# Moving the second block's modulation product from GpSimd in the mixing stage to VectorE in the first feed-forward and down products

## The chip, the cores and the metric

One core of a Trainium2 chip. The metric is the device time of the kernel in microseconds (us), from several executions of the same program. One further execution is recorded by the hardware profiler; its page and its trace are what is read here. Engines: TensorE (PE in the rows, PEld its weight loads), VectorE (DVE), ScalarE (ACT), GpSimd (POOL), and SyncE (SP), which issues transfers. A difference of 0.2% is about what repeated measurements of this kernel can tell from none.

## The reference

Two transformer blocks, one after the other, on a sequence of 512 tokens and 1024 features, all in float32. What matters here:

```
mod = silu(c) @ w_ada + b_ada            # 1024 x 6144 weight, 25 MB, one row
sh1, sc1, g1, sh2, sc2, g2 = split(mod)  # six vectors of 1024
# second block
h = rms_norm(x, norm1_g) * (1 + sc1) + sh1 ... x = x + g1 * (mixed @ w_out)
h = rms_norm(x, norm2_g) * (1 + sc2) + sh2 ... x = x + g2 * (... @ w_down)
# end of the first block, which needs nothing of mod
f = (silu(h @ w_gate) * (h @ w_up)) @ w_down     # 1024 -> 2816 -> 1024
```

So mod depends on c alone, and its first use is the norm at the start of the second block.

## The kernel before

Features lie on partitions, the 512 tokens along the free axis. Weights come as tiles of 1024 x 128 (128 partitions x 8 slices x 128 columns, 512 KB) through three slots. For each tile SP loads `raw` (helper `load`, line 514), ScalarE writes the high part `w_hi` (`split_hi`, line 1102), VectorE the rest `w_lo` (`split_lo`, line 1578), and TensorE does 24 matmuls of 128x128x512: three products for each of 8 slices (line 619, or 806 in the mixing stage). `load` waits until the slot's previous tile has been split (`split_ready`), `split_hi` waits until TensorE has done with the slot (`unit_done`). SP issues its transfers in the order of its program, and each wait there holds all that stands behind it.

The mixing stage of the first block runs in 8 rounds of four or five tiles (`ROUNDS`). In each round TensorE puts projections between the scores, transposes and value products of a pair of heads, VectorE does the score reductions, splits, reciprocals of the gates and norms, and ScalarE the exponentials. Behind the rounds come the products of branch b (line 927), then w_out, norms, the first feed-forward product, the down product, and the second block.

The modulation runs on GpSimd beside these 8 rounds. w_ada is cut into 96 tiles of 64 output features, with the 1024 inputs as 128 partitions x 8; GpSimd loads a tile through its own queue (`ada_load`, line 470, two buffers), multiplies it by cond (line 479), adds in three halvings (lines 482 and 484) into `ada_acc`, and after 12 tiles signals `ada_ready` (line 488). At the end of each round TensorE waits for that signal (`modulation`, line 881) and sums over the partitions with 6 matmuls against ones (12 passes in the rows) into bank O1; VectorE adds the bias (`modulate_out`, line 1790) and frees the bank, and GpSimd begins the next twelve. cond = silu(c) was made early by ScalarE (line 1141) and VectorE (lines 1671 to 1673), with the 1024 features as 128 x 8. Behind the branch products VectorE makes `mod_a` = (1 + sc) * g (lines 1932, 1933).

The first feed-forward product has 22 gate tiles (slot 0) and 22 up tiles (up 0 in slot 2, the others in slot 1). After a first pair, 21 rounds run as a loop on every engine:
- TensorE: up tile j+1 into bank G1, gate tile j+1 into G0.
- VectorE, round j: wait for G1, `cval` (line 1986), `split_lo(1)` of up tile j+2; wait for G0, `cgate` (line 1989), `split_lo(0)` of gate tile j+2; then `fbuf` (line 1970) and, once ScalarE has made f_hi, `f_lo` (line 1973).
- ScalarE: `split_hi(1)`, `split_hi(0)`, silu (line 1399), `f_hi` (line 1401).
- SP, loop of 20 (`ffn_rounds`): load gate tile j+1, load up tile j+2. The gate load waits for the split of gate j, the up load for that of up j+1.

The down product has 8 output tiles of three weight tiles (slots 1, 0, 2 with 8, 8 and 6 slices), accumulated in O0 and O1 by turns; behind each, ScalarE squares and copies it, and VectorE adds the squares and splits the next tile of slot 2.

The waits are counted with semaphores: `w.next(signal, ahead=1)` waits for one use less than the count so far, and `credit=1` lets the first such wait pass. A buffer guarded so is reloaded only after its previous use.

Of the kernel before, what the change touches and what calls it, by code (L numbers as in the profile page):

```python
# [20 lines left out]
F32 = mybir.dt.float32  # L21
F32R = mybir.dt.float32r
I32 = mybir.dt.int32
ACT = mybir.ActivationFunctionType
# [31 lines left out]
def slopes_table():  # L56
# [9 lines left out]
            ("gla_norm_g_2", 1), ("c_2", 8), ("conv_b_2", 44), ("conv_w_2", 132), ("q_norm_g_2", 1), ("k_norm_g_2", 1)]  # L66
# [96 lines left out]
def build(nc, a, out):  # L163
    with ExitStack() as ctx:
# [18 lines left out]
        def signal(name, unit=1, credit=0):  # L183
# [20 lines left out]
        cond = sb("cond", [8])  # L204
        eps6 = sb("eps6", [1])
        eps5 = sb("eps5", [1])
        lamv = sb("lamv", [4, 64])
# [11 lines left out]
        ada_acc = sb("ada_acc", [12, 64])  # L219
# [28 lines left out]
            ("qk", [2, 2, S], F32), ("probs", [2, CAUSAL], F32), ("ada", [2, 8, 64], F32))  # L248
# [37 lines left out]
        ada_flat = ada_acc[:, :, :].rearrange("p a b -> p (a b)")  # L286

# [22 lines left out]
        cond_exp = signal("cond_exp")  # L310
# [40 lines left out]
        ada_used = [signal("ada_used0"), signal("ada_used1")]  # L351
        cond_r = signal("cond_r")
        ada_mm = signal("ada_mm", credit=1)
        ada_ready = signal("ada_ready")
        ada_out = signal("ada_out", credit=1)
# [78 lines left out]
        def _(pool):  # L434
# [33 lines left out]
            def ada_load(t, n):  # L468

                pool.dma_start(ada[:, n, :, :], a["w_ada"][bass.ds(t, 1), :, :]  # L470
                               .rearrange("t p (k c) -> (t p) k c", k=8)).then_inc(ada_in[n], 16)

            def ada_chunk(c, last=False):
                pool.wait_ge(ada_mm, w.next(ada_mm, ahead=1))
                for n in range(12):
                    buf = n % 2
                    chunk = ada[:, buf, :, :]
                    pool.wait_ge(ada_in[buf], w.next(ada_in[buf]))
                    then(pool.tensor_tensor(chunk, chunk, cond[:, :].rearrange("p (k c) -> p k c", c=1).broadcast_to([P, 8, 64]),  # L479
                                            ALU.mult))  # L480
                    for half in (4, 2):
                        then(pool.tensor_tensor(ada[:, buf, 0:half, :], ada[:, buf, 0:half, :],  # L482
                                                ada[:, buf, half:2 * half, :], ALU.add))
                    pool.tensor_tensor(ada_acc[:, n, :], ada[:, buf, 0, :], ada[:, buf, 1, :], ALU.add).then_inc(ada_used[buf], 1)  # L484
                    pool.wait_ge(ada_used[buf], w.next(ada_used[buf]))
                    if n < 10 or not last:
                        ada_load(c * 12 + n + 2, buf)
                pool.sem_inc(ada_ready, 1)  # L488

            for n in range(2):  # L490
                ada_load(n, n)
            pool.wait_ge(cond_r, w.next(cond_r))
# [15 lines left out]
        def _(sp):  # L508
# [66 lines left out]
            ffn_rounds("w_gate", "w_up", 0, "w_down")  # L575
            down_rounds("w_down")
# [25 lines left out]
        def _(pe):  # L602
            w = Waits(pe)
            for free in (v_turned, ada_mm, *unit_done):
                pe.sem_inc(free, 1)
# [268 lines left out]
            def modulation(i):  # L874

                pe.wait_ge(ada_ready, i + 1)
                pe.wait_ge(ada_out, i + 1)
                if i >= 5:
                    pe.wait_ge(o_rs, min(i - 4, 3) if i < 7 else 4)
                for n in range(6):  # L880
                    last = pe.matmul(O1[:, n:n + 1], ada_flat[:, n * P:(n + 1) * P], ones[:, 0:1], start=True, stop=True)  # L881
                last.then_inc(ada_mm, 1)

            for i in range(8):
# [33 lines left out]
                modulation(i)  # L918
# [170 lines left out]
        def _(act):  # L1089
# [44 lines left out]
            for n in range(4):  # L1134
# [5 lines left out]
                if n == 1:  # L1140
                    act.activation(cond[:, :], cols[:, VEC_AT["c_2"]:VEC_AT["c_2"] + 8], ACT.Exp, scale=-1.0).then_inc(cond_exp, 1)
# [1117 lines left out]
```

## Time and profile before

| | us |
|---|---|
| median of 3 runs | 1629.0 (1628.54 to 1630.68) |
| the profiled execution, its own time | 1627.7 |
| its span in the profile | 1626.0 |
| TensorE busy | 1445.8 (89%) |
| VectorE busy | 860.0 (53%) |
| ScalarE busy | 580.6 (36%) |
| GpSimd busy | 353.9 (22%), all within the first 482 us |
| transfers | 146.19 MB, mean 90 GB/s |
| mean granted clock of TensorE | 0.944 of full speed |

Busy time is a share over stages with different limits; an engine's idle time costs only where the chain that ended last runs through it. The profile lists for each group of instructions the idle time of its engine just before it and what ended that, and for any stretch the busy time of each engine and the granted clock of TensorE. Matmul ends are modelled and overlap the next start, so 0.39 us of duration go with 0.227 from start to start at full clock.

### The profile page before, as it was taken

To read this page: it belongs to the slowest core of one execution; us is meant where nothing else is said; L and a number is where in the kernel's file an instruction comes from. 1 tells how busy PE (TensorE), PEld (TensorE's weight loads), DVE (VectorE), ACT (ScalarE), POOL (GpSimd) and SP (SyncE) were. 2 spreads that over 40 slices of the span, in tenths; PEclk is the share of its full clock that TensorE was granted. 3 is DMA by queue.
4 is the path that set the end of the run, shared out by engine and by line. 5 is a ranking of instruction groups with operands and counts; after the bars stand their busy time and mean duration, and the time that the engine had idled before them with its cause. 6 is when DMAs were issued, how large, how long until landed. Compare 5 with 4: busy or idle time off the path is not lost.

```text
span 1626.0 us, 19342 instructions
## 1 busy us (share of the span) xinstructions
PE 1445.8 (89%) x6538; PEld 1147.0 (71%) x6538; DVE 860.0 (53%) x1299; ACT 580.6 (36%) x917; POOL 353.9 (22%) x511
## 2 busy tenths in 40 slices
PE   7994586668678899999999889989979999999999
PEld 6773464456456678888888668866757788888887
DVE  5863354566457635444422368755554656565321
ACT  5441232233233433232322362444423544444221
POOL 5867777777750000000000000000000000000000
PEclk9996887788789999999999989999999999999999
DMA  5443332333312122222333121211102132323332
GB/s 193 138 126 89 102 110 84 105 110 96 104 54 96 62 90 91 100 93 97 97 107 94 61 79 52 78 39 39 52 13 101 64 103 90 103 91 100 111 94 87
DMA packets 42176, 146.19 MB, mean 90 GB/s; under 512 B 5376, under 2 KB 5648, under 8 KB 42128
## 3 DMA queue, kind: packets, MB, share of 16 engines
q1 hardware_dynamic: 34448, 120.39, 22.4%
q0 software_dynamic: 7680, 25.17, 5.4%
q8 instruction: 29, 0.48, 0.1%
q14 instruction: 19, 0.16, 0.0%
HBM read 143.44 MB, written 2.10 MB: 90 GB/s over the span
## 4 chain that ended last, share of the span: by engine, by line
PE 70%; POOL 15%; issue 7%; DVE 4%; ACT 1%; DMA 1%; POOLq 1%; DVEq 0%; SPq 0%; ACTq 0%
PE bank L619 55%; POOL ada L482 7%; POOL ada L479 5%; PE bank L763 3%; PE bank L654 2%; POOL ada_acc L484 2%; PE bank L806 1%; PE bank L1023 1%; PE bank L881 1%; PE bank L735 1%; PE bank L927 1%; PE bank L669 1%; PE bank L726 1%; PE bank L641 1%; POOL ada L470 1%
## 5 line engine op out<-in xcount | busy, mean ns | idle before, releaser
L1578 DVE TENSOR_TENSOR w_lo<-raw,w_hi 128x1024 fp32r<-128x1024 f32 (+1 forms) x225 | 278.3, 1239 | 199.4 <-ACT w_hi L1102 198.0
L619 PE MATMUL bank<-h_hi,w_hi 128*128 128x512 f32 x872 | 345.6, 396 | 0.8 <-DVE gyf L2122 0.8
L1102 ACT ACTIVATE w_hi<-raw 128x1024 fp32r<-128x1024 f32 (+1 forms) x225 | 233.4, 1039 | 308.1 <-PE bank L619 287.4
L619 PE MATMUL bank<-h_lo,w_hi 128*128 128x512 f32 x872 | 340.4, 390 | 0.0
L619 PE MATMUL bank<-h_hi,w_lo 128*128 128x512 f32 x872 | 340.2, 390 | 0.0
L619 PEld LDWEIGHTS bank<-h_hi,w_hi 128*128 128x128 f32 x872 | 164.0, 188 | 42.2 <-issue 7.1
L619 PEld LDWEIGHTS bank<-h_hi,w_lo 128*128 128x128 f32 x872 | 164.1, 188 | 34.7
L619 PEld LDWEIGHTS bank<-h_lo,w_hi 128*128 128x128 f32 x872 | 164.3, 188 | 32.7 <-issue 0.2
L619 PE MATMUL bank<-f_hi,w_lo 128*128 128x512 f32 x352 | 137.0, 389 | 0.0
L619 PE MATMUL bank<-f_lo,w_hi 128*128 128x512 f32 x352 | 137.0, 389 | 0.0
L619 PE MATMUL bank<-f_hi,w_hi 128*128 128x512 f32 x352 | 137.0, 389 | 0.0
L482 POOL TENSOR_TENSOR ada<-ada 128x256 f32<-128x256 f32 x192 | 131.6, 686 | 15.1
L881 PE MATMUL bank<-ones,ada_acc 128*128 128x1 f32 x96 | 20.4, 340 | 112.5 <-POOLq L488 112.5
L479 POOL TENSOR_TENSOR ada<-ada,cond 128x512 f32<-128x512 f32 x96 | 103.9, 1082 | 25.2 <-PE bank L881 19.5
L806 PE MATMUL bank<-h_hi,w_hi 128*128 128x512 f32 x240 | 102.4, 427 | 0.3 <-DVE ma L1774 0.3
L502 POOL IOTA mj<- 128x128 int32 x1 | 0.2, 234 | 470.2 <-DVE gacc L2020 470.2
L881 PEld LDWEIGHTS bank<-ones,ada_acc 128*128 128x128 f32 x96 | 19.9, 312 | 115.5 <-POOLq L488 115.5
L806 PE MATMUL bank<-h_hi,w_lo 128*128 128x512 f32 x240 | 96.7, 403 | 0.0
L806 PE MATMUL bank<-h_lo,w_hi 128*128 128x512 f32 x240 | 96.6, 403 | 0.0
L1178 ACT ACTIVATE probs<-probs,negmaxs 128x128 f32<-128x128 f32 (+3 forms) x64 | 35.4, 554 | 163.2 <-DVE negmaxs L1723 163.2
L619 PEld LDWEIGHTS bank<-f_hi,w_hi 128*128 128x128 f32 x352 | 66.1, 188 | 13.8
L619 PEld LDWEIGHTS bank<-f_lo,w_hi 128*128 128x128 f32 x352 | 66.1, 188 | 13.7
(297 smaller groups left out, 2188.3 us busy)
## 6 DMA issues: line engine op xcount, KB each, us to landing
raw<-in_w_up SPq DMA_DIRECT2D x66, 512.0 KB, 3.3
raw<-in_w_mix SPq DMA_DIRECT2D x48, 512.0 KB, 3.4
ada<-in_w_ada POOLq DMA_DIRECT2D x96, 256.0 KB, 3.0
raw<-in_w_down SPq DMA_DIRECT2D x32, 512.0 KB, 3.5
raw<-in_w_in SPq DMA_DIRECT2D x25, 512.0 KB, 3.3
raw<-in_w_gate SPq DMA_DIRECT2D x22, 512.0 KB, 3.3
raw<-in_w_out SPq DMA_DIRECT2D x16, 512.0 KB, 3.3
raw<-in_w_down SPq DMA_DIRECT2D x16, 384.0 KB, 3.2
```

The source lines that it names most:

```text
L470: pool.dma_start(ada[:, n, :, :], a["w_ada"][bass.ds(t, 1), :, :] .rearrange("t p (k c) -> (t p) k c", k=8)).then_inc(ada_in[n], 16)
L479: then(pool.tensor_tensor(chunk, chunk, cond[:, :].rearrange("p (k c) -> p k c", c=1).broadcast_to([P, 8, 64]), ALU.mult))
L482: then(pool.tensor_tensor(ada[:, buf, 0:half, :], ada[:, buf, 0:half, :], ada[:, buf, half:2 * half, :], ALU.add))
L484: pool.tensor_tensor(ada_acc[:, n, :], ada[:, buf, 0, :], ada[:, buf, 1, :], ALU.add).then_inc(ada_used[buf], 1)
L619: last = pe.matmul(to[:, :], wt[:, slot, k, :], act_[:, rhs0 + k, :], start=(k == first and n == 0), stop=(k == K - 1 and n == 2))
L654: last = pe.matmul(to[g][:, :], wt[:, slot, k, :], act_[:, k, :], start=(k == 0 and n == 0), stop=(k == KU - 1 and n == 2))
L763: last = pe.matmul(banks[r][:, :], xt[:, k, P * r:P * r + P], wt[:, slot, 4 * kk:4 * kk + 4, :].rearrange("p a b -> p (a b)"), start=(k == ...
L806: last = pe.matmul(G[u % 2][:, :], wt[:, slot, k, :], act_[:, kr, :], start=(kr == 0 and m == 0), stop=(kr == length - 1 and m == 2))
L881: last = pe.matmul(O1[:, n:n + 1], ada_flat[:, n * P:(n + 1) * P], ones[:, 0:1], start=True, stop=True)
L1102: act.activation(w_hi[:, s, 0:K, :], raw[:, s, 0:K, :], ACT.Copy).then_inc(hi_ready[s], 1)
L1178: act.activation(probs[:, m, p:p + P * (r + 1)], probs[:, m, p:p + P * (r + 1)], ACT.Exp, scale=-1.0, bias=negmaxs[:, r, m:m + 1], accum_o ...
L1578: dve.tensor_tensor(w_lo[:, s, 0:K, :], raw[:, s, 0:K, :], w_hi[:, s, 0:K, :].bitcast(F32), ALU.subtract).then_inc(split_ready[s], 1)
```

## The change

The modulation leaves GpSimd, TensorE and the mixing stage. The weight is stored transposed, as 48 blocks of 128 output features x 1024 inputs with the features on partitions, and c is stored broadcast to all partitions (128 x 1024). A block comes in two halves of 128 x 512 (256 KB each), loaded by SP. VectorE takes each half with one product-and-sum instruction against cond and adds the two sums into one column of `modc`. Blocks 0 to 41 go two to a round of the feed-forward loop, blocks 42 to 47 with the first six output tiles of the down product. `ada` has one buffer for each half, and SP's loads of them stand between the tile loads of the same queue. ScalarE makes cond with one Silu. The bias and mod_a are made before the norm behind the down product. In the mixing stage all waits for the modulation go; where bank O1 was freed by them, a wait for `o_rs` stands instead.

```diff
         ada_in = [signal("ada_in0", 16), signal("ada_in1", 16)]
-        ada_used = [signal("ada_used0"), signal("ada_used1")]
+        ada_used = [signal("ada_used0", credit=1), signal("ada_used1", credit=1)]
+        cond_in = signal("cond_in", 16)
...
@@ GpSimd
-            def ada_load(t, n):
-                pool.dma_start(ada[:, n, :, :], a["w_ada"][bass.ds(t, 1), :, :]
...
-            with w.repeat(7, {ada_in[0]: 6, ada_in[1]: 6, ada_used[0]: 6, ada_used[1]: 6, (ada_mm, 1): 1, step: 36}) as c:
-                ada_chunk(c)
-            ada_chunk(7, last=True)
...
@@ SP
-            def ffn_rounds(gate, up, up0, down):
+            def ada_load(t):
+
+                for half in range(2):
+                    sp.wait_ge(ada_used[half], w.next(ada_used[half], ahead=1))
+                    sp.dma_start(ada[:, half, :], a["w_ada"][bass.ds(t, 1), :, half * S:half * S + S]
+                                 .rearrange("t p k -> (t p) k")).then_inc(ada_in[half], 16)
+
+            def ffn_rounds(gate, up, up0, down, modulation=False):
 
                 load(0, tile(gate, 0))
                 load(1, tile(up, up0 + 1))
                 down_unit(down, 0, 2)
-                with w.repeat(NF - 2, {(split_ready[0], 1): 1, (split_ready[1], 1): 1}) as j:
+                more = {}
+                if modulation:
+                    sp.dma_start(cond[:, :], a["c_2"]).then_inc(cond_in, 16)
+                    more = {(ada_used[0], 1): 2, (ada_used[1], 1): 2}
+                with w.repeat(NF - 2, {(split_ready[0], 1): 1, (split_ready[1], 1): 1, **more}) as j:
                     load(0, tile(gate, j + 1))
+                    if modulation:
+                        ada_load(j * 2)
                     load(1, tile(up, j + (up0 + 2)))
+                    if modulation:
+                        ada_load(j * 2 + 1)
                 load(0, tile(gate, NF - 1))
+                if modulation:
+                    ada_load(2 * NF - 4)
 
-            def down_rounds(name):
+            def down_rounds(name, modulation=False):
 
                 down_unit(name, 0, 1)
+                if modulation:
+                    ada_load(2 * NF - 3)
                 down_unit(name, 0, 0)
+                if modulation:
+                    ada_load(2 * NF - 2)
                 for c in range(1, KD):
                     for s in DOWN:
                         down_unit(name, c, s)
+                        if modulation and s == 0 and c <= 5:
+                            ada_load(2 * NF - 2 + c)
...
@@ TensorE, mixing stage
                 pe.wait_ge(o_sq, i - 3)
-                pe.wait_ge(ada_out, min(i + 1, 7) + 1)
+                pe.wait_ge(o_rs, i - 4) if i >= 5 else None
...
-                modulation(i)
...
@@ ScalarE
             gated(0, gate_pre)
+            act.wait_ge(cond_in, w.next(cond_in))
+            act.activation(cond[:, :], cond[:, :], ACT.Silu).then_inc(cond_r, 1)
...
@@ VectorE, mixing stage
-                modulate_out(i)
...
@@ VectorE, feed-forward loop
+            def modulation(t, parity):
+
+                for half in range(2):
+                    dve.wait_ge(ada_in[half], w.next(ada_in[half]))
+                    dve.tensor_tensor_reduce(ada[:, half, :], ada[:, half, :], cond[:, half * S:half * S + S], 1.0, 0.0,
+                                             ALU.mult, ALU.add, ada_sum[:, parity, half:half + 1]).then_inc(ada_used[half], 1)
+                for half in range(2):
+                    dve.wait_ge(ada_used[half], w.next(ada_used[half]))
+                dve.tensor_tensor(modc[:, bass.ds(t, 1)], ada_sum[:, parity, 0:1], ada_sum[:, parity, 1:2],
+                                  ALU.add).then_inc(mod_sum[parity], 1)
...
                 split_lo(1)
+                modulation(j * 2, 0)
                 dve.wait_ge(unit_done[0], w.next(unit_done[0]))
...
                 finish_f(j + 1)
+                modulation(j * 2 + 1, 1)
...
+            def square_and_modulation(g, c):
+
+                add_squares(g)
+                modulation(c + 2 * NF - 2, g)
...
+            for parity in range(2):
+                dve.wait_ge(mod_sum[parity], 24)
+            then(dve.tensor_tensor(modc[:, :], modc[:, :], cols[:, VEC_AT["b_ada_2"]:VEC_AT["b_ada_2"] + 48], ALU.add))
+            for n, name in enumerate(("norm1_g_2", "norm2_g_2")):
+                then(dve.tensor_scalar(mod_a[:, n, :], modc[:, 24 * n + 8:24 * n + 16], 1.0, None, ALU.add))
+                then(dve.tensor_tensor(mod_a[:, n, :], mod_a[:, n, :], cols[:, VEC_AT[name]:VEC_AT[name] + 8], ALU.mult))
             post_norm(oT, lambda k: col("norm_ffn_post_g", k))
```

The block number of a round is the same on both sides: SP's loop step j loads blocks 2j and 2j+1, VectorE's loop step j uses them.

## Rows read from the trace of the kernel before

**Rows 1.** The chain that ended last, shares of the span by engine.
```profile
PE 70%; POOL 15%; issue 7%; DVE 4%; ACT 1%; DMA 1%; POOLq 1%; DVEq 0%; SPq 0%; ACTq 0%
```

**Rows 2.** Costliest groups: count | busy, mean ns of one | idle before, releaser.
```profile
L881 PE MATMUL bank<-ones,ada_acc 128*128 128x1 f32 x96 | 20.4, 340 | 112.5 <-POOLq L488 112.5
```

**Rows 3.** Stretches of the mixing stage: length, busy by engine, granted clock, DMA share, GB/s.
```profile
70.27:473.67 403.40, 284.10 (x1264) 213.59 (x1265) 207.36 (x321) 128.33 (x277) 305.49 (x449) 0.83 0.33 103
...
99.03:128.96 29.93, 29.93 (x149) 22.02 (x148) 21.87 (x38) 13.75 (x32) 23.83 (x34) 1.00 0.40 123
...
150.41:185.80 35.39, 35.38 (x160) 26.62 (x160) 22.30 (x38) 13.33 (x31) 26.46 (x38) 0.88 0.33 104
...
204.47:238.52 34.05, 34.05 (x160) 25.68 (x160) 21.75 (x38) 13.34 (x31) 25.11 (x38) 0.91 0.34 105
```

**Rows 4.** The same view over the feed-forward product and most of the down product.
```profile
577.00:925.00 348.00, 348.00 (x1536) 288.03 (x1535) 143.81 (x163) 105.16 (x129) 0.00 (x0) 1.00 0.30 95
```

**Rows 5.** Timeline, end of the last mixing round: start, length, instruction.
```profile
459.38 1.02 PE L872 MATMUL bank<-sqacc,ones 128*128 128x512 f32 x2
...
467.70 1.29 DVE L1774 TENSOR_TENSOR ma<-bank,gate_a 128x512 f32<-128x512 f32 x2
```

**Rows 6.** TensorE's waits from 370 to 475 us: total, times, longest.
```profile
PE bank L845 <- DVE probs L1746: 6.5, 3, 3.3
```

**Rows 7.** Groups on VectorE, mixing stage, as rows 2.
```profile
L1739 DVE TENSOR_TENSOR nlams<-rrows,lams 128x1 f32<-128x1 f32 x16 | 9.7, 606 | 0.6
...
L1790 DVE TENSOR_TENSOR modc<-bank,cols 128x6 f32<-128x6 f32 x8 | 1.3, 165 | 120.9 <-PE bank L881 120.9
```

**Rows 8.** Timeline on VectorE, attention of the second block.
```profile
1108.54 0.68 DVE L1905 CUSTOM_DVE_ANT_0 prob<-prob,seen 128x512 f32<-128x512 f32 x1
...
1109.15 0.68 DVE L1905 CUSTOM_DVE_ANT_0 prob<-prob,seen 128x512 f32<-128x512 f32 x1
...
1109.96 0.17 DVE L1909 RECIPROCAL rrow<-rowsum 128x2 f32<-128x2 f32 x1
```

**Rows 9.** Timeline of one feed-forward round, VectorE, then ScalarE.
```profile
649.18 1.23 DVE L1578 TENSOR_TENSOR w_lo<-raw,w_hi 128x1024 fp32r<-128x1024 f32 x1 [0.40 <-ACT w_hi L1102]
653.53 0.69 DVE L1989 TENSOR_TENSOR cgate<-bank,rstd 128x512 f32<-128x512 f32 x1 [3.12 <-PE bank L619]
654.62 1.23 DVE L1578 TENSOR_TENSOR w_lo<-raw,w_hi 128x1024 fp32r<-128x1024 f32 x1 [0.40 <-ACT w_hi L1102]
655.76 0.68 DVE L1970 TENSOR_TENSOR fbuf<-cval,sil 128x512 f32<-128x512 f32 x1
657.45 0.69 DVE L1973 TENSOR_TENSOR f_lo<-fbuf,f_hi 128x512 f32 x1 [1.00 <-ACT f_hi L1401]
658.97 0.69 DVE L1986 TENSOR_TENSOR cval<-bank,rstd 128x512 f32<-128x512 f32 x1 [0.83 <-PE bank L619]
...
658.97 1.06 ACT L1102 ACTIVATE w_hi<-raw 128x1024 fp32r<-128x1024 f32 x1 [1.75 <-PE bank L619]
```

**Rows 10.** SP's issues: two in a row at 486 us, one in that round.
```profile
486.50 0.88 SPq L514 DMA_DIRECT2D raw<-in_w_out  x2
...
650.68 0.33 SPq L514 DMA_DIRECT2D raw<-in_w_up  x1
```

**Rows 11.** DMA issues (all; from 319.5, 813.5, 486): KB, median us to landing.
```profile
raw<-in_w_gate SPq DMA_DIRECT2D x22, 512.0 KB, 3.3
...
raw<-in_w_mix SPq DMA_DIRECT2D x1, 512.0 KB, 3.5
...
raw<-in_w_down SPq DMA_DIRECT2D x1, 512.0 KB, 4.6
...
raw<-in_w_out SPq DMA_DIRECT2D x2, 512.0 KB, 7.6
```

**Rows 12.** VectorE's first loop f_lo of that stage and its last.
```profile
592.17 0.69 DVE L1973 TENSOR_TENSOR f_lo<-fbuf,f_hi 128x512 f32 x1 [1.01 <-ACT f_hi L1401]
...
809.76 0.69 DVE L1973 TENSOR_TENSOR f_lo<-fbuf,f_hi 128x512 f32 x1 [1.00 <-ACT f_hi L1401]
```

**Rows 13.** SP's waits over the whole span: total, times, longest.
```profile
SPq L514 <- DVE w_lo L1578: 1443.9, 212, 38.5
```

More of the change, by code:

```diff
@@ L203, in build @@
         mod_a = sb("mod_a", [2, 8])
[L204 removed]
+        ada_sum = sb("ada_sum", [2, 2])
         eps6 = sb("eps6", [1])
         eps5 = sb("eps5", [1])
[L207 removed]
         lams = sb("lams", [8])
@@ L218, in build @@
         rcol = sb("rcol", [NT])
-        ada_acc = sb("ada_acc", [12, 64])
+        cond = sb("cond", [D])
         osq = sb("osq", [2])
@@ L466, in _ @@
             differences(idiff1)
-            def ada_load(t, n):
-                pool.dma_start(ada[:, n, :, :], a["w_ada"][bass.ds(t, 1), :, :]
[L471 to L492, printed above, removed]
-            with w.repeat(7, {ada_in[0]: 6, ada_in[1]: 6, ada_used[0]: 6, ada_used[1]: 6, (ada_mm, 1): 1, step: 36}) as c:
-                ada_chunk(c)
-            ada_chunk(7, last=True)
             pool.wait_ge(yb_ready, KD)
@@ L603, in _ @@
             w = Waits(pe)
-            for free in (v_turned, ada_mm, *unit_done):
+            for free in (v_turned, *unit_done):
                 pe.sem_inc(free, 1)
@@ L1560, in _ @@
             w = Waits(dve)
-            for free in (q_taken, k_taken, y_f32, *sq_used, f_f32, conv_gd, conv_vd, *drained_x, ada_out, gate_read, up_read,
+            for free in (q_taken, k_taken, y_f32, *sq_used, f_f32, conv_gd, conv_vd, *drained_x, *ada_used, gate_read, up_read,
                          y_ready, f_ready, *split_ready, gy_ready):
@@ L1669, in _ @@
                 scaled_lo(k)
-            dve.wait_ge(cond_exp, w.next(cond_exp))
-            then(dve.tensor_scalar(cond[:, :], cond[:, :], 1.0, 3e38, ALU.add, ALU.min))
-            then(dve.reciprocal(cond[:, :], cond[:, :]))
-            dve.tensor_tensor(cond[:, :], cond[:, :], cols[:, VEC_AT["c_2"]:VEC_AT["c_2"] + 8], ALU.mult).then_inc(cond_r, 1)
             split_lo(2)
@@ L1928, in _ @@
             staging = {hi_ready[s]: 1 for s in range(3)}
-            dve.wait_ge(ada_out, w.next(ada_out, times=8))
-            for n, name in enumerate(("norm1_g_2", "norm2_g_2")):
-                then(dve.tensor_scalar(mod_a[:, n, :], modc[:, 24 * n + 8:24 * n + 16], 1.0, None, ALU.add))
-                then(dve.tensor_tensor(mod_a[:, n, :], mod_a[:, n, :], cols[:, VEC_AT[name]:VEC_AT[name] + 8], ALU.mult))
             two = {hi_ready[0]: 1, hi_ready[1]: 1}
@@ L1994, in _, with down @@
                 finish_f(j + 1)
-            def down(each, more, last=None, follows=False):
+                modulation(j * 2 + 1, 1)
+            def down(each, more, last=None, follows=False, seventh=None):
                 per = {**{hi_ready[s]: 2 for s in range(3)}, **more}
@@ L2010, in down @@
                             else:
-                                each(g, 6 + g)
+                                (seventh or each)(g, 6 + g)
                         if g == 0 or follows and s < 2:
@@ L2016, in _ @@
             split_lo(2, K=6)
-            down(lambda g, c: add_squares(g), sums, skip_last_square, follows=True)
+            def square_and_modulation(g, c):
+                add_squares(g)
+                modulation(c + 2 * NF - 2, g)
+            down(square_and_modulation, {**sums, ada_in[0]: 2, ada_in[1]: 2, ada_used[0]: 2, ada_used[1]: 2}, skip_last_square, follows=True,
+                 seventh=lambda g, c: add_squares(g))
+            for parity in range(2):
[4 more added lines that the diff above has]
+                then(dve.tensor_tensor(mod_a[:, n, :], mod_a[:, n, :], cols[:, VEC_AT[name]:VEC_AT[name] + 8], ALU.mult))
             post_norm(oT, lambda k: col("norm_ffn_post_g", k))
```

36 lines of the change are left out of this document (12 added, 24 removed).

## The prediction

> **What bounds the kernel now.** I read the chain of waits first: TensorE holds 70% of it, but GpSimd 15% [rows 1]. So some stretch is set by GpSimd. The costliest groups name it: the matmuls of line 881, which turn the modulation's partial sums, cost 20.4 us themselves, and TensorE sat idle for 112.5 us until GpSimd's counter of line 488 [rows 2]. Third, the stretches of the mixing stage. From its first round to the branch products it lasts 403.4 us, at a mean granted clock of 0.83. The second round ran at 1.00 throughout and took 29.9 us. The third and fourth have the same work and took 35.4 and 34.1, of which 2.7 are their line 881, so 32.7 and 31.3: after each idle time TensorE comes back at its lower level (1.2 GHz, against 2.4) and the start of the round is paid at that [rows 3]. In the first feed-forward product TensorE never waits: 1536 matmuls in 348.0 us at 1.00, so 48 of them, one round, take 10.88 us [rows 4]. That is the stage which receives the work.
>
> **What the mixing stage gives back.** 112.5 us of idle time and 20.4 us of line 881 [rows 2]. Lower clock: 2.8 and 1.4 us in the two rounds above; with a mean of 2.1, six restarts make 12.8, and I add 3 for the low stretches after stalls in the last two rounds: 15.6. Together 148.5. Two things go the other way or are uncertain. The last round's end was covered by GpSimd: from the squares at 459.4 VectorE needs until 469.0 for norm, low part, reciprocal and the two products that free the banks, while TensorE's own fill ends at 465.2 [rows 5]. So 3.2 us of new wait stand at the branch products. The stalls for attention weights (6.5 us, [rows 6]) become smaller: one-column VectorE operations took 606 ns beside GpSimd, a six-column one 165 ns when GpSimd stood still [rows 7]. But VectorE comes later into each round now, since it no longer rests 15 us; I keep 3 us of stall (0 to 7). Net 148.5 - 3.2 + 3.5 = 148.8 us. The branch products start at a higher clock: 1 us. cond and the small operations that go from VectorE early, and those of mod_a that go behind the branch products, lie beside matmuls: nothing either way. The six small ones that come before the post norm fall into the wait for rstd: nothing.
>
> **What the VectorE work costs by itself.** A product-and-sum of 128x512 in SBUF follows its like at 0.61 us, and a dependent small operation ends 1.6 us after the first began [rows 8]. So one block of 128 features is 1.6 us, two per round 3.2. VectorE's part of a round has 3.1 us free between the two splits and some 0.8 at the end [rows 9]. By time alone it fits; a split may be 3 us late before TensorE sees it. If only this counted, the stage would cost nothing.
>
> **What it costs in the queue of loads.** This is the term that decides. SP issues in order and a wait holds everything behind it. Before, the tile of the next-but-one round is asked for as soon as VectorE has split the one before: the split ends at 650.40, the load is issued at 650.68, and it is wanted by ScalarE 8 us later, at 658.97 [rows 9, 10]. Now the loop of SP is: gate tile, block 2j, up tile, block 2j+1. Each half of ada has one buffer, so block 2j waits until VectorE has used block 2j-1, the last thing in VectorE's round j-1; and the up tile behind it is the very one that VectorE splits first in round j. Likewise the gate tile stands behind block 2j+1, which waits for block 2j, just ahead of the gate's split. The prefetch distance is gone, and two load latencies lie in a closed ring. From the start of the second block of a round (0):
> - halves used at 0.69 and 1.30; two issues of 0.33 us and the way through SP (0.2 to 0.3 behind a release, 0.54 from issue to issue, [rows 10]): up tile issued at 2.2.
> - landing. Alone it takes 3.3 to 3.4 us; behind a modulation load on the other queue 3.5, behind a 384 KB load on its own 4.6 [rows 11]. Here 512 KB are just ahead: I take 3.9, ends 3.3 and 4.6. Landed 6.1.
> - ScalarE's high part 1.06 and VectorE's low part 1.23 with their gaps [rows 9]: 8.4.
> - first block: halves used at 9.1 and 9.7, loop end of SP, gate tile issued at 10.7; landing 3.7 (the halves are further ahead): 14.4.
> - both parts again 16.8; fbuf 0.68, then 1.00 of wait for f_hi and 0.69 for f_lo [rows 9]: 19.05, and the next block starts.
>
> So a round takes 19.05 us instead of 10.88: 20 times 8.17 = 163.4. In the first round block 0's use delays gate 2, and f_lo ends near 597.5 instead of 592.9 [rows 12]: 4.7. At the end, TensorE ran 10.4 us past VectorE's last f_lo of 810.45 [rows 12]; now it starts the first down tile late and ends 7.3 behind it: -3.1. Its restarts at the lower level add 1.5. Sum for the stage 166.5. TensorE itself is busy 10.9 of 19 us, so even with half of it at the lower level it doesn't close the ring.
>
> By the fit of the Trainium skill (DMA: Bandwidth & Descriptors, section "Anatomy of one DMA": 2.0 us plus bytes over 436 GB/s) the tile would land about 3.2 us behind its issue even after the two halves, and the ring would be 1.2 us shorter, 24 us in all; that fit is for the GpSimd path.
>
> **Down product.** One block for each of six output tiles. The third weight tile is now issued behind the load that waits for the block, about 3.5 us after the output tile is done; landed at 7, split at 9, wanted at 10.9. Slack 2 us where there were 8. At the entry the first tile is about a microsecond late. I take 2 (0 to 8, for straggling loads: the two issued behind another at 486 needed 7.6, [rows 11]).
>
> **Sum.** -148.8 - 1 + 166.5 + 2 = +18.7, against the profiled execution of 1627.7 us (span 1626.0 and 1.7 around it): 1646.4. That execution is 1.3 under the median of 1629.0, so 1647.7 for the median; I say 1647.
>
> **Rivals.** (a) Shorter ring, faster in the end. Same mechanism, other size: it decides at 18.1 us a round, since each microsecond of ring is 20 us. With 3.3 us landings behind everything the ring is 18.05 and the kernel at 1628; with SP half a microsecond quicker besides, 17.8 and 1623. For it: most loads land at 3.3. Against: none of those had 512 KB ahead. 0.12. (b) The change doesn't bring the ring: the loads stay ahead, and only the VectorE time counts. Then 1629 - 149.8 + 2 = 1481. It needs SP not to be held by the waits; against it, 1444 us of SP's time are such waits already, for splits [rows 13]. 0.04. The Trainium skill (DMA: Bandwidth & Descriptors, section "Anatomy of one DMA") has a semaphore wait happen on the issuing sequencer before dispatch; by that, (b) can't be. (c) TensorE closes the ring: idle twice a round, it stays at 1.2 GHz, 48 matmuls take up to 21.8 us, and the stage costs 55 more: 1702; half of that effect 1675. For it: the granted clock was 0.88 and 0.91 in rounds that began after an idle time, 1.00 in the one that did not [rows 3]. Against: the ring gives each unit some 3 us of room. 0.08. (d) The forecast: 0.76.
>
> **Chances and range.** A measurement here tells 0.2% (3.3 us) from no change. Case (a) splits into faster 0.06 and same 0.06, (b) is faster; the rest is slower: 0.10, 0.06, 0.84. The range: landings of 3.3 give 1627, of 4.6 (ring 20.6) 1678, and the mixing stage holds 4 us more each way: 1623 to 1682.
>
> **What would show it.** In the changed profile the idle time of line 881 is gone, the mixing stage is near 255 us at a clock near 1.00, and VectorE's one-column operations there near 0.2 us. In the feed-forward product the granted clock drops, line 619 waits for w_lo (VectorE) some 40 times, 7 to 8 us a round, and the ring of 19 us shows between two f_lo. SP's up and gate loads come right behind ada loads. Wrong would be: 10.9 us between two f_lo (then (b)), or TensorE busy throughout the ring (then (c)), or new stalls over 7 us in the mixing rounds.

## The result and the profile after

The changed kernel takes 1671.85 us (median of 4 runs, 1666.73 to 1672.27) against 1629.4 for the kernel before (4 runs on the same chip): a ratio of 1.0253, 95% interval 1.0231 to 1.0274. It is slower by 42.5 us, where the forecast was 18. The profiled execution has a span of 1670.5 us, 44.5 more than the one of before, at a mean granted clock of 0.946.

First the changed kernel's chain by engine, which answers to [rows 1]. In the second line the columns are engine, line and share.

```profile
PE 63%; DMA 12%; DVE 10%; issue 6%; ACT 6%; SPq 1%; DVEq 0%; ACTq 0%
PE bank L611 38%; PE bank L798 10%; DMA raw<-in_w_gate 5%; DMA raw<-in_w_up 5%; ACT w_hi L1083 3%; DVE ada L1952 3%; PE bank L755 3%; PE bank L646 2%; PE bank L819 1%; DMA raw<-in_w_down 1%; PE bank L1004 1%; PE bank L727 1%; SPq L528 1%; DVE fbuf L1935 1%; PE bank L908 1%
```

GpSimd's 15% are gone. In their place stand DMA with 12% where it had 1%, VectorE with 10% where it had 4, ScalarE with 6 where it had 1. The two new lines of 5% are loads of exactly the tiles that used to arrive unseen. That is the picture of a ring that passes through all three: load, high part, low part, modulation, load.

The stretches say where the time went. Mixing (from 70.76), branch products and w_out (324.44), first feed-forward product up to the end of the first down tile (406.24), the seven other down tiles (861.22); columns as in [rows 3].

```profile
70.76:324.44 253.68, 248.63 (x1169) 183.77 (x1169) 179.66 (x314) 127.12 (x277) 1.75 (x4) 1.00 0.21 69
324.44:406.24 81.80, 72.46 (x293) 57.40 (x293) 51.51 (x63) 27.60 (x41) 0.00 (x0) 0.94 0.28 95
406.24:861.22 454.98, 332.46 (x1138) 252.26 (x1138) 182.59 (x362) 85.49 (x108) 0.00 (x0) 0.85 0.31 99
861.22:969.03 107.81, 105.39 (x464) 86.85 (x464) 40.67 (x65) 29.83 (x37) 0.00 (x0) 1.00 0.37 123
```

The feed-forward stretch of the kernel before, in the same columns:

```profile
556.54:820.90 264.36, 264.36 (x1140) 215.58 (x1141) 127.73 (x154) 86.38 (x109) 0.00 (x0) 0.99 0.28 91
```

Mixing took 403.4 before [rows 3] and takes 253.7 now, -149.7, at a granted clock of 1.00 throughout. The feed-forward stretch took 264.4 before and takes 455.0, +190.6, at 0.85. The second stretch is 1.1 shorter, the down tiles 3.2 longer (104.6 before), all the rest together 1.5 longer: -149.7 - 1.1 + 190.6 + 3.2 + 1.5 = 44.5.

TensorE's waits in the feed-forward stretch (total, times, longest), then in the mixing stage; the second group answers to [rows 2] and [rows 6].

```profile
PE bank L611 <- DVE w_lo L1560: 122.5, 41, 5.5
PE bank L646 <- DVE h_lo L1604: 5.7, 1, 5.7
```

```profile
PE bank L908 <- DVE ma L1752: 3.3, 1, 3.3
PE bank L837 <- DVE probs L1724: 1.2, 1, 1.2
```

In a stage where it never waited, TensorE now waits 41 times for the low part of a weight tile. (The 5.7 us for h_lo end at the border of the stretch and were there before.) In mixing, the 112.5 us for GpSimd are gone and one new wait of 3.3 us stands at the branch products.

One turn of the ring, from the timeline of the changed kernel between 569 and 592 us: SP's issues, the steps of VectorE and ScalarE that lie in the ring, and the two matmuls that waited. The rows between them are left out. (Start, length, instruction; in brackets the idle time before it and its releaser.)

```profile
569.18 0.69 DVE L1938 TENSOR_TENSOR f_lo<-fbuf,f_hi 128x512 f32 x1 [1.00 <-ACT f_hi L1381]
569.79 0.68 DVE L1952 CUSTOM_DVE_ANT_0 ada<-ada,cond 128x512 f32<-128x512 f32 x1
570.41 0.68 DVE L1952 CUSTOM_DVE_ANT_0 ada<-ada,cond 128x512 f32<-128x512 f32 x1
570.66 0.93 SPq L528 DMA_DIRECT2D ada<-in_w_ada  x2
571.79 0.33 SPq L483 DMA_DIRECT2D raw<-in_w_up  x1
576.36 1.06 ACT L1083 ACTIVATE w_hi<-raw 128x1024 fp32r<-128x1024 f32 x1 [7.41 <-DMA raw<-in_w_up]
577.45 1.23 DVE L1560 TENSOR_TENSOR w_lo<-raw,w_hi 128x1024 fp32r<-128x1024 f32 x1 [5.04 <-ACT w_hi L1083]
578.59 0.68 DVE L1952 CUSTOM_DVE_ANT_0 ada<-ada,cond 128x512 f32<-128x512 f32 x1
578.73 0.51 PE L611 MATMUL bank<-h_hi,w_hi 128*128 128x512 f32 x1 [3.71 <-DVE w_lo L1560]
579.45 0.94 SPq L528 DMA_DIRECT2D ada<-in_w_ada  x2
581.02 0.33 SPq L483 DMA_DIRECT2D raw<-in_w_gate  x1
585.75 1.06 ACT L1083 ACTIVATE w_hi<-raw 128x1024 fp32r<-128x1024 f32 x1 [8.34 <-DMA raw<-in_w_gate]
586.84 1.23 DVE L1560 TENSOR_TENSOR w_lo<-raw,w_hi 128x1024 fp32r<-128x1024 f32 x1 [5.95 <-ACT w_hi L1083]
588.12 0.50 PE L611 MATMUL bank<-h_hi,w_hi 128*128 128x512 f32 x1 [2.05 <-DVE w_lo L1560]
589.67 0.69 DVE L1938 TENSOR_TENSOR f_lo<-fbuf,f_hi 128x512 f32 x1 [1.01 <-ACT f_hi L1381]
```

Read it as a loop. VectorE uses the two halves of a modulation block (569.79, 570.41); that lets SP issue the next two halves, and only behind them the up tile (571.79). ScalarE waits for it until 576.36, VectorE until 577.45, and only then comes the next block (578.59), which frees the gate tile (581.02), and so on. Nothing in the ring is TensorE: over the 20 turns (447 to 853 us) no wait of VectorE, ScalarE or SP ends on it. These are the longest of theirs:

```profile
DVE w_lo L1560 <- ACT w_hi L1083: 215.5, 40, 6.0
ACT w_hi L1083 <- DMA raw<-in_w_gate: 155.5, 19, 8.4
SPq L528 <- DVE ada_sum L1952: 329.9, 42, 9.8
```

TensorE's two waits of 3.71 and 2.05 us hang on the ring from outside. Some time after each of them its matmuls run at the lower level (1.2 GHz) for 3 us or more, 0.43 us from start to start for 0.23, as two matmuls of the same turn show:

```profile
570.08 0.63 PE L611 MATMUL bank<-h_hi,w_lo 128*128 128x512 f32 x1
...
573.00 0.40 PE L611 MATMUL bank<-h_lo,w_hi 128*128 128x512 f32 x1
```

From f_lo to f_lo it is 20.49 us here; over the 20 periods of the loop the mean is 20.28 (19.7 to 20.6), against 10.88 before.

Last, the issues and landings of the changed kernel from 450 to 850 us; they answer to [rows 11].

```profile
ada<-in_w_ada SPq DMA_DIRECT2D x78, 256.0 KB, 3.0
raw<-in_w_up SPq DMA_DIRECT2D x19, 512.0 KB, 4.5
raw<-in_w_gate SPq DMA_DIRECT2D x19, 512.0 KB, 4.5
```

Each tile lands 4.5 us behind its issue, with the two halves of a block just ahead of it. Before, it was 3.3.

### The profile page after: what moved, and what is told of

Read it like the earlier page. It is cut to its first block, busy times and chain, and to the rows that moved or that the text cites. A ratio compares the mean times of both kernels' runs of the same rounds, so it can differ in the third digit from the quotient of the medians.

```text
span 1670.5 us, 18837 instructions
## 1 busy us (share of the span) xinstructions
PE 1479.9 (89%) x6442; PEld 1154.9 (69%) x6442; DVE 887.8 (53%) x1529; ACT 580.6 (35%) x917; POOL 18.3 (1%) x31
## 4 chain that ended last, share of the span: by engine, by line
PE 63%; DMA 12%; DVE 10%; issue 6%; ACT 6%; SPq 1%; DVEq 0%; ACTq 0%
PE bank L611 38%; PE bank L798 10%; DMA raw<-in_w_gate 5%; DMA raw<-in_w_up 5%; ACT w_hi L1083 3%; DVE ada L1952 3%; PE bank L755 3%; PE bank L646 2%; PE bank L819 1%; DMA raw<-in_w_down 1%; PE bank L1004 1%; PE bank L727 1%; SPq L528 1%; DVE fbuf L1935 1%; PE bank L908 1%
## 5 line engine op out<-in xcount | busy, mean ns | idle before, releaser
L1560 DVE TENSOR_TENSOR w_lo<-raw,w_hi 128x1024 fp32r<-128x1024 f32 (+1 forms) x225 | 272.4, 1212 | 400.0 <-ACT w_hi L1083 398.4
L611 PE MATMUL bank<-h_hi,w_hi 128*128 128x512 f32 x872 | 373.7, 429 | 116.4 <-DVE w_lo L1560 115.7
L611 PE MATMUL bank<-h_lo,w_hi 128*128 128x512 f32 x872 | 361.8, 415 | 0.0
L611 PE MATMUL bank<-h_hi,w_lo 128*128 128x512 f32 x872 | 360.3, 413 | 0.0
L611 PEld LDWEIGHTS bank<-h_hi,w_hi 128*128 128x128 f32 x872 | 177.0, 203 | 177.9 <-DVE w_lo L1560 132.2
L611 PEld LDWEIGHTS bank<-h_hi,w_lo 128*128 128x128 f32 x872 | 177.1, 203 | 40.7
L611 PEld LDWEIGHTS bank<-h_lo,w_hi 128*128 128x128 f32 x872 | 178.1, 204 | 36.2 <-issue 0.2
L798 PE MATMUL bank<-h_hi,w_hi 128*128 128x512 f32 x240 | 98.5, 410 | 0.5 <-DVE ma L1752 0.4
L798 PE MATMUL bank<-h_hi,w_lo 128*128 128x512 f32 x240 | 93.9, 391 | 0.0
L798 PE MATMUL bank<-h_lo,w_hi 128*128 128x512 f32 x240 | 93.5, 390 | 0.0
L611 PEld LDWEIGHTS bank<-f_hi,w_lo 128*128 128x128 f32 x352 | 66.4, 189 | 13.8
L1952 DVE CUSTOM_DVE_ANT_0 ada<-ada,cond 128x512 f32<-128x512 f32 x96 | 62.3, 686 | 1.0 <-DVE sqacc L1576 1.0
L798 PEld LDWEIGHTS bank<-h_hi,w_hi 128*128 128x128 f32 x240 | 45.1, 188 | 20.9 <-issue 13.2
L1938 DVE TENSOR_TENSOR f_lo<-fbuf,f_hi 128x512 f32 (+1 forms) x44 | 30.5, 693 | 43.9 <-ACT f_hi L1528 22.0
L798 PEld LDWEIGHTS bank<-h_hi,w_lo 128*128 128x128 f32 x240 | 45.0, 188 | 10.1
L798 PEld LDWEIGHTS bank<-h_lo,w_hi 128*128 128x128 f32 x240 | 45.2, 188 | 8.0
```

The lines of the kernel that those rows point to most:

```text
L611: last = pe.matmul(to[:, :], wt[:, slot, k, :], act_[:, rhs0 + k, :], start=(k == first and n == 0), stop=(k == K - 1 and n == 2))
L798: last = pe.matmul(G[u % 2][:, :], wt[:, slot, k, :], act_[:, kr, :], start=(kr == 0 and m == 0), stop=(kr == length - 1 and m == 2))
L1560: dve.tensor_tensor(w_lo[:, s, 0:K, :], raw[:, s, 0:K, :], w_hi[:, s, 0:K, :].bitcast(F32), ALU.subtract).then_inc(split_ready[s], 1)
L1938: dve.tensor_tensor(at_k(f_lo, j), fbuf[:, :], at_k(f_hi, j).bitcast(F32), ALU.subtract).then_inc(f_ready, 1)
L1952: dve.tensor_tensor_reduce(ada[:, half, :], ada[:, half, :], cond[:, half * S:half * S + S], 1.0, 0.0, ALU.mult, ALU.add, ada_sum[:, parit ...
```

## The experiments

The theory on trial: SP issues in order, so a tile load that stands behind a modulation load inherits its wait for VectorE; two load latencies then lie in a closed ring, and the length of the ring sets the time. The rivals: VectorE's added work makes the round longer; the added traffic makes the tiles late; or TensorE at its lower clock closes the ring. Four runs ask which of these it is, four more what the ring consists of, and one how much VectorE could take. The edits are given in short, with constants put in; lines that only keep the counts right are left out.

### The loads on GpSimd's queue

```
     block.gpsimd:
             differences(idiff)
+            with w.repeat(48, {(ada_used[0], 1): 1, (ada_used[1], 1): 1}) as t:
+                for half in range(2):
+                    pool.wait_ge(ada_used[half], w.next(ada_used[half], ahead=1))
+                    pool.dma_start(ada[:, half, :], a["w_ada"][bass.ds(t, 1), :, half * S:half * S + S]
+                                   .rearrange("t p k -> (t p) k")).then_inc(ada_in[half], 16)
     block.sync: all calls of ada_load taken out
```

> Edit: the 96 modulation loads leave SP and are issued by GpSimd, which is idle by then; VectorE's instructions, the single buffer, the bytes and the packets stay. Theory (SP's queue is held: each tile load stands behind a load that waits for VectorE's last block): the tiles are again asked for a round ahead, the ring of 20.25 us between two f_lo goes back to about 10.9, the first feed-forward stage from 455.0 to about 265, and the kernel to 1629.4 - 149.7 - 1.1 + 1.0 + about 3 for the down product = 1483 us (1478 to 1492). Rival VectorE (its added work, not the queue, makes the round longer): the two blocks of 1.6 us stay, 20 rounds by 3.2 = 64 more, 1545 or higher, and with its waits unchanged 1672. Rival traffic (1 MB of modulation in each round slows the tiles that share the DMA engines): the tiles still land 4.5 us behind their issue and the kernel stays above 1600.

Measured: 1476.3 us (4 runs, 1473.9 to 1477.1), ratio to the kernel before 0.907 (0.905 to 0.909). The ring is 10.88 us between two f_lo. Its loads and landings, 450 to 640 us:

```profile
ada<-in_w_ada POOLq DMA_DIRECT2D x70, 256.0 KB, 3.2
raw<-in_w_up SPq DMA_DIRECT2D x17, 512.0 KB, 3.3
raw<-in_w_gate SPq DMA_DIRECT2D x17, 512.0 KB, 3.2
```

Same bytes, same VectorE instructions, same single buffer, and the 195 us to the changed kernel are gone. What has changed is the queue on which the wait is made and, with it, the moment at which each tile is issued. The time lies 2 us below the range I gave: the 3 us that I had added for the down product didn't come (from the last f_lo to the end it is 816.0 us here and 816.2 in the kernel before). Both rivals on VectorE and on traffic needed 1545 or more.

### The same queue, the tiles a round ahead

```
     def ffn_rounds, with modulation:
+        load(0, tile(gate, 1))
+        load(1, tile(up, up0 + 2))
-        with w.repeat(NF - 2, ...) as j:
-            load(0, tile(gate, j + 1))
+        with w.repeat(NF - 3, ...) as j:
+            load(0, tile(gate, j + 2))
             ada_load(j * 2)
-            load(1, tile(up, j + (up0 + 2)))
+            load(1, tile(up, j + (up0 + 3)))
             ada_load(j * 2 + 1)
```

with the blocks that are left over placed behind the last gate tile and the first two tiles of the down product.

> Edit: SP keeps all loads and ada keeps its single buffer; only the order changes: each modulation block is issued one round (two tiles) later in SP's list, so that no tile stands behind a block which VectorE uses after that tile's predecessor. Theory (queue): a tile is asked for a round ahead again; a block has from the end of one use to the start of the next, 5.45 - 1.6 = 3.85 us when TensorE paces, and needs about 0.5 + 3.0 = 3.5: ring 10.9 to 11.5 us, kernel 1483 us (1479 to 1500). Rival VectorE: at least 1545, as in the run with the loads on GpSimd. Rival traffic: same bytes on the same queue, still above 1600.

Measured: 1475.7 us (4 runs, 1474.5 to 1479.9), ratio 0.906 (0.905 to 0.908), ring 10.87; 3 us below the range I gave. Timeline of VectorE and SP in this kernel, rows between left out:

```profile
560.67 0.69 DVE L1943 TENSOR_TENSOR f_lo<-fbuf,f_hi 128x512 f32 x1 [1.00 <-ACT f_hi L1386]
561.28 0.69 DVE L1957 CUSTOM_DVE_ANT_0 ada<-ada,cond 128x512 f32<-128x512 f32 x1
563.80 1.22 DVE L1565 TENSOR_TENSOR w_lo<-raw,w_hi 128x1024 fp32r<-128x1024 f32 x1
571.55 0.69 DVE L1943 TENSOR_TENSOR f_lo<-fbuf,f_hi 128x512 f32 x1 [1.01 <-ACT f_hi L1386]
```

```profile
562.15 0.94 SPq L528 DMA_DIRECT2D ada<-in_w_ada  x2
565.20 0.33 SPq L483 DMA_DIRECT2D raw<-in_w_up  x1
565.79 0.94 SPq L528 DMA_DIRECT2D ada<-in_w_ada  x2
570.24 0.33 SPq L483 DMA_DIRECT2D raw<-in_w_gate  x1
```

The tile load now comes as soon as the split of its slot is done (the split ends at 565.02, the load is issued at 565.20), as in the kernel before [rows 9, 10]. The two f_lo are 10.88 us apart. So the order of the loads in one queue is worth 196 us of 1672, with all data, all work and all buffers as they were.

### The same by half as much

```
     def ffn_rounds, with modulation: prologue as above, then
+            ada_load(j * 2)
+            load(0, tile(gate, j + 2))
+            ada_load(j * 2 + 1)
+            load(1, tile(up, j + (up0 + 3)))
```

> Edit: the same shift by half as much: every modulation block is issued one tile later than in the changed kernel, not two. A tile is then issued right behind the block that waits for the end of VectorE's last use, and is split one half round later. Theory (queue): from the end of a block's use 0.9 to issue, 4.5 to land, 2.3 for both splits = 7.7 us, where TensorE's pace gives 5.45 + 2.3 = 7.8: it just fits or costs a few tenths in each half, ring 10.9 to 12.5 us, kernel 1483 to 1520, say 1492. Rivals as in the other two runs: VectorE at least 1545, traffic above 1600.

Measured: 1482.8 us (4 runs, 1481.9 to 1484.4), ratio 0.911 (0.909 to 0.912), ring 11.17 (10.87 to 11.59), where 1492 (from 1483) had been expected. Its loads from 450 to 640 us:

```profile
ada<-in_w_ada SPq DMA_DIRECT2D x68, 256.0 KB, 3.2
raw<-in_w_gate SPq DMA_DIRECT2D x17, 512.0 KB, 4.4
raw<-in_w_up SPq DMA_DIRECT2D x17, 512.0 KB, 4.6
```

This run separates latency from hold. The tiles land as late as in the changed kernel, 4.4 to 4.6 us, and each still stands behind a load that waits for VectorE, yet the kernel is 7 us from the best. Half a round more between issue and use leaves room for nearly all of it: the round is 0.3 us over TensorE's 10.88. In the changed kernel, where nothing is left between them, it is 9.4.

### No modulation loads at all

```
     block.sync: all calls of ada_load taken out
     block.vector:
-                    dve.wait_ge(ada_in[half], w.next(ada_in[half]))
+            then(dve.memset(ada[:, :, :], 0.0))      (once, ahead of the loop)
```

> Edit: the modulation loads are left out (ada is set to zero once, so the modulation is the bias alone); all of VectorE's product-and-sum instructions stay. It gives the price of VectorE's work by itself and a floor for the two runs that keep the loads. Theory (queue): VectorE's 3.2 us per round lie beside TensorE, ring 10.9 us, 1481 us (1478 to 1486). Rival VectorE: 64 us above that or as slow as the changed kernel, 1545 to 1672. Rival traffic: also about 1481, so the difference to the GpSimd run would be the price of the traffic: the theory says under 5 us, the rival more than 100.

Measured: 1477.1 us (4 runs, 1475.9 to 1478.0), ratio 0.907 (0.906 to 0.909), ring 10.85; 1 us below the range I gave. Without the 25 MB of loads the kernel is no faster than with them on GpSimd's queue or in the better order. Neither the traffic nor VectorE's 3.2 us a round cost anything that a run can show, so I see nothing of the change's own cost left in the kernels of 1476 us.

### Short product-and-sum instructions, loads as in the change

```
-  dve.tensor_tensor_reduce(ada[:, half, :], ada[:, half, :], cond[:, half * S:half * S + S], 1.0, 0.0,
+  dve.tensor_tensor_reduce(ada[:, half, 0:8], ada[:, half, 0:8], cond[:, half * S:half * S + 8], 1.0, 0.0,
```

> Edit to the changed kernel: all loads, their order and all waits stay; the product-and-sum instructions cover 8 columns of each half instead of 512 (so the modulation is a part of the true sum). In the ring as measured, VectorE's work counts from the start of the block to the use of its second half, 1.30 us, twice a round; with 8 columns I estimate 0.45 from the 0.16 us of the small addition and its gaps. Theory (queue ring): 20.25 - 2 x 0.85 = 18.6 us a round and 1672 - 34 = 1638 us. Rival VectorE: without its work the rounds are as before, 10.9 us and about 1480. In between, a ring of 17.0 (1608 us) would say that the whole 1.6 us of each block lie in the ring.

Measured: 1646.3 us (2 runs, 1646.0 and 1646.6), ratio 1.0115 (1.009 to 1.015), ring 19.15. The rival is out by 166 us: nearly all of VectorE's work for the modulation taken away, and the kernel is still slower than before. My own 18.6 us for the ring is 0.55 too low, and my 1638 for the kernel 8 too low. The trace tells why: the up tile is issued 1.40 us behind the block's start, where it was 2.00. Only 0.60 of the 0.85 is saved, because SP needs 0.53 from one half's issue to the next, and the halves are now free faster than SP can issue.

### Half the columns loaded

```
-  sp.dma_start(ada[:, half, :], a["w_ada"][bass.ds(t, 1), :, half * S:half * S + S] ...
+  sp.dma_start(ada[:, half, 0:256], a["w_ada"][bass.ds(t, 1), :, half * S:half * S + 256] ...
```

> Edit to the changed kernel: each modulation load brings 256 of its 512 columns (128 rows of 1 KB), the rest of ada is zero; same number of loads and rows, same waits, half the bytes. The step of the prediction that missed is the landing of a tile behind the two halves, 4.5 us measured where 3.3 is the value without company. If the bytes ahead make the 1.2 us, half of them make 0.6: landing 3.9, ring 20.25 - 1.2 = 19.05 us, kernel 1648. If the number of rows ahead makes it, landing 4.5, ring 20.2, kernel 1672.

### One load for each block

```
   sp.wait_ge for both halves, then
+  sp.dma_start(ada[:, :, :].rearrange("p h c -> p (h c)"), a["w_ada"][bass.ds(t, 1), :, :] ...).then_inc(ada_in[0], 16)
```

> Edit to the changed kernel: one load of 512 KB (128 rows of 4 KB) for each block in place of two of 256 KB (rows of 2 KB), issued when both halves are used. Bytes the same, rows half as many, one issue less. If the bytes ahead make the landing: 4.5 us or some tenths more, since nothing of the block can start earlier; ring 20.2 to 20.8, kernel 1670 to 1683. If the rows or the number of loads make it: landing 3.9, ring 19.05, kernel 1648.

### A quarter of the rows loaded

```
+  sp.dma_start(ada[0:32, half, :], a["w_ada"][bass.ds(t, 1), 0:32, half * S:half * S + S] ...
```

> Edit to the changed kernel: each modulation load brings 32 of its 128 rows (2 KB each), the rest of ada is zero; same number of loads, same waits, a quarter of the bytes and of the rows. What is left is the hold of the queue with nearly no traffic behind it. Theory (queue ring): landing 3.3 + 0.3 = 3.6 us, ring 20.25 - 1.8 = 18.45 us, kernel 1636: the hold makes some 7.5 of the 9.4 us that a round lost, the bytes the rest. Rival traffic (the bytes themselves hold up the stage): a quarter of the loss, ring about 13.2, kernel about 1530.

These three ask what makes the landing of the tile late. The landings from 450 to 640 us, for half the columns, for one load per block, and for a quarter of the rows:

```profile
ada<-in_w_ada SPq DMA_DIRECT2D x40, 128.0 KB, 2.4
raw<-in_w_gate SPq DMA_DIRECT2D x10, 512.0 KB, 3.9
raw<-in_w_up SPq DMA_DIRECT2D x9, 512.0 KB, 3.9
```

```profile
ada<-in_w_ada SPq DMA_DIRECT2D x19, 512.0 KB, 3.3
raw<-in_w_gate SPq DMA_DIRECT2D x10, 512.0 KB, 4.5
raw<-in_w_up SPq DMA_DIRECT2D x9, 512.0 KB, 4.1
```

```profile
raw<-in_w_up SPq DMA_DIRECT2D x11, 512.0 KB, 3.3
raw<-in_w_gate SPq DMA_DIRECT2D x11, 512.0 KB, 3.3
ada<-in_w_ada SPq DMA_DIRECT2D x43, 64.0 KB, 1.8
```

| kernel | KB ahead of a tile | tile lands after (gate, up) | ring | span | median |
|---|---|---|---|---|---|
| the change | 512, 2 loads | 4.5, 4.5 | 20.28 | 1670.5 | 1671.9 |
| one load per block | 512, 1 load | 4.5, 4.1 | 20.07 | 1661.4 | 1662.8 (2 runs) |
| short product-and-sum | 512, 2 loads | 4.6, 4.4 | 19.15 | 1644.9 | 1646.3 (2 runs) |
| half the columns | 256, 2 loads | 3.9, 3.9 | 18.95 | 1643.8 | 1639.6 (4 runs, 1638.8 to 1645.6) |
| a quarter of the rows | 128, 2 loads | 3.3, 3.3 | 18.01 | 1622.5 | 1622.0 (7 runs) |

In these loops landing follows the bytes ahead. Half the bytes in as many rows and loads give 3.9, as expected from bytes (ring 18.95 for 19.05; the median of 1640 is 8 below the 1648 expected, and the profiled execution, from which ring and landings are read, is the slowest of its four); the same bytes in half the rows and one load less give 4.1 to 4.5, mostly as expected from bytes (the ring of 20.07 lies just below the 20.2 to 20.8 I gave, and the time 7 us below). At 128 KB ahead the delay is gone altogether, where I had expected 0.3: 18.01 for 18.45, and 1622 for 1636. From the last row to the first the span grows by 48.0 us for 2.27 us of ring: 21 us for each microsecond. The 20 periods make 45.4 of the 48.0; of the rest, 3.5 lie behind the last f_lo, and the first round goes the other way.

The last row is also the verdict on traffic. With a quarter of the modulation's bytes a round still takes 18.01 us. So the hold of the queue, with landings of 3.3 us in it, makes 7.1 of the 9.4 us that a round lost, and the bytes that delay the tile the other 2.3. The rival's 13.2 us and 1530 are out.

### Twice the product-and-sum instructions, in the better order

```
     def modulation(t, parity), in the kernel with the tiles a round ahead:
+                more(0)                                (a product-and-sum of 128x512 that nothing needs)
                 for half in range(2): ...
+                then(more(1))
```

> Edit to the kernel with the tiles issued a round ahead (1475.7 us): each modulation block gets two more product-and-sum instructions of 128x512 that nothing needs, so VectorE's work for the modulation is doubled. In that kernel one round of VectorE, added up from start to start, is f_lo 0.61, block 1.92, cval 0.60, low part 1.14, block 1.9, cgate 0.60, low part 1.14, fbuf and the wait for f_hi 1.68: about 9.6 of 10.88 us. Theory (VectorE's time is hidden until its own list is longer than TensorE's round): two blocks grow by 1.4 each, list 12.4, ring 12.2 to 12.6 us, kernel 1475.7 + 20 x 1.5 = 1506 (1500 to 1512). Rival: the splits may slip 3 us and blocks overlap with waits, so it stays hidden: 10.9 and 1476. Rival VectorE as a bound of its own from the start would have shown in the runs before.

Measured: 1504.4 us (2 runs, 1503.6 and 1505.2), ratio 0.924 (0.922 to 0.927), ring 12.09 (12.08 to 12.12). TensorE's waits, 406 to 861 us:

```profile
PE bank L618 <- DVE w_lo L1567: 19.7, 22, 1.6
```

VectorE as the bound looks like this: one short wait a round, the same each time, and a round just as long as VectorE's own list. The theory's 1506 is met within 2 us; its ring lies 0.1 below the lower end of 12.2 to 12.6. Four instructions at 0.61 us from start to start were added; the rest of the list, its wait for f_hi included, is then at most 12.09 - 2.44 = 9.65 of 10.88 us. VectorE has at least 1.2 us a round free with the change's work in it.

## Why the prediction missed

**Mixing stage: right.** -148.8 forecast, -149.7 measured, and its parts too: the idle time and the matmuls of line 881 are gone, and TensorE's other busy time fell by 15.1 us (284.10 - 20.4 - 248.63), where 15.6 had been put down to the lower clock. The new wait at the branch products was put at 3.2 us and is 3.3 (it ends with the first of the two products, at about 468.4 in the kernel before, and not with the second at 469.0, which the prediction names beside it). Stalls on the attention weights were kept at 3 and are 1.2. The one-column operations on VectorE went from 606 ns [rows 7] to 159 with GpSimd out of the way, as the argument had it. This is the changed kernel's group:

```profile
L1717 DVE TENSOR_TENSOR nlams<-rrows,lams 128x1 f32<-128x1 f32 x16 | 2.5, 159 | 0.6
```

**Branch products: right**, -1.1 for -1.

**VectorE's work by itself: right**, hidden: the run without loads is the evidence, and the run with twice the products shows how near the edge it is.

**The ring: right in kind, too short.** This is the step that failed: "landing. Alone it takes 3.3 to 3.4 us; behind a modulation load on the other queue 3.5, behind a 384 KB load on its own 4.6. Here 512 KB are just ahead: I take 3.9", and "landing 3.7 (the halves are further ahead)" for the gate tile. Measured, mean of 17 turns in the middle of the stage (20.32; over all 20 it is 20.28), from the block's start, with landing counted to the start of ScalarE's high part:

| step | forecast | measured |
|---|---|---|
| block's start to issue of the up tile | 2.2 | 2.00 |
| landing of the up tile | 3.9 | 4.52 |
| high part, low part | 2.3 | 2.23 |
| first block to issue of the gate tile | 2.3 | 2.41 |
| landing of the gate tile | 3.7 | 4.62 |
| both parts, fbuf, f_hi, f_lo | 4.65 | 4.54 |
| sum | 19.05 | 20.32 |

The four terms of VectorE, ScalarE and SP came from rows and stand within 0.2 us. Both landings were chosen between a row of 3.3 and one of 4.6, and I leaned to the lower. The row of 4.6 was nearer in kind: same queue, a load of like size just ahead. So was the one of 7.6, which I used for the down product alone: the first of its two tiles had one 512 KB tile 0.7 us ahead and landed after 7.2. At the same place in the changed kernel it is 5.0, with the loads on GpSimd's queue 4.4. No run says where that spread comes from; bytes ahead are not all of it. The two landings are 1.5 us too short, the other terms 0.3 too long, together 1.27; 20 turns make 25 us, and the stage's miss is 190.6 - 166.5 = 24.1. The stated upper end of the range (landing 4.6, ring 20.6, 1678) is 6 us above what came. The reason I gave for a shorter gate landing is refuted: the gate's halves are issued 1.58 and 0.97 us ahead of it, the up tile's 1.13 and 0.53, and it lands no sooner than the up tile.

**First round and down product.** First round +5.3 (13.7 us between the first two f_lo for 8.4) where 4.7 was forecast; down tiles +3.2 for 2, inside its 0 to 8. With 20 rounds at +9.4, what is left of the stage's +190.6 is -2.7, where -1.6 was forecast for its end and restarts.

**Sum.** -149.7 for -148.8, -1.1 for -1, +190.6 for +166.5, +3.2 for +2, +1.5 for 0 in the rest: 44.5 for 18.7 on the profiled executions. A net effect of two large terms with opposite sign is hostage to the less certain one: 15% of the feed-forward term is more than the whole forecast.

**The rivals.** (a) A ring of 18.05 or less and a time no worse than before: not with this change's bytes, but the turning point was placed well. The run with a quarter of the rows has a ring of 18.01 and takes 1622.0, ratio 0.996; at 21 us for each microsecond that puts break-even near 18.3, for 18.1 forecast. (b) Loads stay ahead, 1481: not for this change; with another order of the same queue it is 1476. The Trainium skill's statement (DMA: Bandwidth & Descriptors, section "Anatomy of one DMA") that a semaphore wait is made on the issuing sequencer before dispatch agrees with the runs: with the wait on GpSimd's queue in place of SP's the tiles are no longer held, 1476.3 us for 1671.9. The same section's fit for loads on GpSimd's path, 2.0 us plus bytes over 436 GB/s, gives as an estimate 3.2 us for a 512 KB tile; SP's tiles take 3.3 without company and 4.5 behind 512 KB, so here the measurement decides. (c) TensorE closes the ring: no. It waits 41 times, and nothing in the ring waits for it (the waits above), so its lower clock adds nothing to the round. It takes 20.28 - 122.5 / 20 = 14.2 us for the matmuls that took 10.88, which is why the waits came to 6.1 us a round instead of the 7 to 8 forecast, and the ring of VectorE, ScalarE and SP runs on unmoved.

## What to carry to other kernels

Before a wait is put into an in-order queue, ask which later entries stand behind it and how far ahead of their use they were issued. If the wait depends on the engine that also uses those entries, prefetch turns into a closed ring, and its length is the sum of the latencies and of the short steps between them, not the busy time of any engine. Place each load in the queue in the order in which its buffer becomes free, not in the order in which the data are used; here that alone turned 1672 us into 1476, 9.4% under the kernel before, with nothing else changed. Where the answer is a small difference of large terms, take the most uncertain term from the row nearest in kind, and let the range lean that way.

## What was not expected of the hardware

A 512 KB tile's landing went with what had been issued 0.5 to 1.6 us ahead of it on the same queue: 3.3 us with nothing or 128 KB, 3.9 with 256 KB, 4.1 to 4.6 with 512 KB. With 512 KB whose last load lay 2.4 us or more ahead (the tiles a round ahead) it was 3.2 to 3.3. It is no law of bytes: a w_out tile 0.7 us behind a 512 KB tile took 7.2 us in the kernel before and 5.0 in the changed one. In the changed kernel the first of the tile's 16 increments comes 3.3 us behind the issue (2.9 before) and the last 4.5 (3.3 before), so the spread among them grows more than the start. With the modulation loads on GpSimd's queue, the nearest of them 1.5 to 2.4 us away from a tile's issue, the tiles landed at 3.2 to 3.3. GpSimd took 540 ns to issue such a load and SP 330. The 96 loads on GpSimd did not slow VectorE's 128x512 product-and-sum: 690 ns, against 686 in the changed kernel. Whether the same bytes issued on the other queue at the same moment as a tile would delay it too wasn't tried.
